# Half of the branch product moved between the steps of the sparse attention, with its gated chunks kept in DRAM, and a new order of some MLP work

## The chip, the cores and the metric

The kernel runs as one program on one core of a Trainium2 chip. The metric is the device time of one execution in microseconds (us). Before the change three runs gave 1763.05, 1754.05 and 1754.68 us, with a median of 1754.68 us. The profiled execution took 1753.3 us.

## The reference, cut to what matters

The program is one decoder layer on 1040 positions (16 meta tokens and 1024 of the input), with a width of 1024. A normalised input is projected; stick-breaking attention (8 heads, "SB") and indexer-selected sparse attention (8 heads, "DS") run on it; their outputs go through one branch matrix each, are gated per channel, summed and projected; then comes a squared-ReLU MLP.

```python
    o_sb = jnp.transpose(o_sb, (1, 0, 2, 3, 4)).reshape(b, tp, SB_W).astype(h.dtype)
    o_ds = jnp.transpose(o_ds, (1, 0, 2, 3, 4)).reshape(b, tp, DSA_W).astype(h.dtype)
    gates = jax.nn.sigmoid(jnp.concatenate([g_sb, g_ds], axis=-1) + b_gate)
    gate_sb, gate_ds = gates[..., :D_MODEL], gates[..., D_MODEL:]
    merged = gate_sb * (o_sb @ w_branch_sb) + gate_ds * (o_ds @ w_branch_dsa)
    return merged @ w_out
...
        h = h + rms_norm(mix, g_mix_post[l])
        ff = sq_relu_mlp(rms_norm(h, g_mlp_pre[l]), w_mlp_in[l], w_mlp_out[l])   # u = relu(h @ w1); (u * u) @ w2
        h = h + rms_norm(ff, g_mlp_post[l])
```

Only `gate_sb * (o_sb @ w_branch_sb)` is moved in time by the change. It needs the SB heads alone, and these are finished before the DS heads start.

## The kernel before, in words

Every matrix product is made to near fp32 accuracy by three passes: each operand is split into a rounded part (`_hi`) and the rest (`_lo`), and TensorE adds hi·hi, hi·lo and lo·hi into one PSUM bank. ScalarE writes the `_hi` parts, and GpSimd or VectorE subtracts to get the `_lo` parts. Weights come in units of 128 x 1024 numbers (512 KB): SyncE loads one (`load_unit`), ScalarE rounds it (`round_unit`), GpSimd takes the rest (`rest_unit`). There are two buffers for them.

The second block of the program holds the projections and the attention. Its order is written out by hand as steps j = 0 to 132, and every engine has its own loop over the same steps. A job is one head and one block of 128 queries; the eight blocks of a head come in the order 7, 0, 6, 1, 5, 2, 4, 3, so a head is eight steps. Steps 0 to 63 start the SB jobs, steps 64 to 127 the DS jobs; head g starts in step 8g. In a step TensorE does, in this order: the scores of job j (`scores`, lines 759 and 760, in two PSUM banks that VectorE empties at line 1163), products of weights and values (`product`, line 810), projection work in the first 64 steps (`project`), the transposes of the weights of job j-2 (`turn`, line 775), once per head the transposes of the next head's values (`values`, line 741), more projection work, and more products. The groups of transposes take turns in PSUM banks 4, 5, 6, and from step 66 on bank 0 too (`tp_take`). ScalarE rounds each group out of its bank (line 932), VectorE takes the rest (line 1192), and the bank is free then. From step 64 on TensorE has no projection work between these.

SyncE issues all DMAs of the block in one queue, in order, and its waits hold back all that stand behind them. `load_head` brings queries, keys and values of a head by eight DMAs and stands in the step after the one that starts the head before. The SB outputs lie in DRAM in two halves; at the steps RELOAD[p] (70, 80, 90, 100) SyncE loads two halves for a pair of heads in `o_raw` (line 648), GpSimd adds them in the step after (line 681), ScalarE rounds the sum at the end of the third step after (`reload`, line 967), GpSimd takes the rest (line 684), and only then may the next pair be loaded, since the buffer is the same.

The third block starts with the branch product: for each of eight chunks k of 128 channels TensorE runs 48 matmuls of 512 columns (24 for SB, 24 for DS; line 344). VectorE multiplies both results by their gates (lines 1891 and 1892), GpSimd adds them (line 1529), ScalarE rounds the sum, and VectorE takes the rest (line 1897). Then come the output projection with norms and residual (lines 1578 and 1596), and the MLP. Both MLP products are made with seven smaller products in place of eight (Strassen-Winograd), so sums of weights and of results are made beside them. The first is a loop over k = 0 to 55 (`inner`, line 1651, 12 matmuls each), the second a loop over i = 0 to 27 (`outer`, line 1674, 48 matmuls each, in four tiles). In both each engine works down its own list. `inner_add` (line 2021) adds a result out of PSUM, `f_sums` (lines 2032 to 2035) makes sums for the second product, `fourth_raw` (lines 2005 and 2007) a difference of activations, `diff_rest` (line 1538, GpSimd) its `_lo` part, `outer_add` (line 2121) adds a tile into `acc`, `last_norm` (lines 2132, 2126, 2136) scales a finished row block of the upper half, and `right_gain`, `left_gain` and `final_row` do so for the lower half.

Of the kernel before, what the change touches and what calls it, by code (L numbers as in the profile page):

```python
# [20 lines left out]
P = 128  # L21
# [23 lines left out]
U_BRANCH, U_OUT, U_MLP = 43, 51, 59  # L45
# [82 lines left out]
RELOAD = [NJ // 2 + 6 + 10 * p_ for p_ in range(4)]  # L128
# [11 lines left out]
def tp_take(key, j):  # L140

    ring = (4, 5, 6) if j < NJ // 2 + 2 else (4, 5, 6, 0)
    TPN[key] = len(TP_BANK)
    TP_BANK.append(min(ring, key=lambda b: max([n for n, x in enumerate(TP_BANK) if x == b], default=-1)))
# [107 lines left out]


# [21 lines left out]
def build(nc, x, meta, w_units, b_gate, g_pre, g_post, g_mlp_pre, g_mlp_post, ident, strict, fill,  # L275
          rope_i, rope_d, out):
    with ExitStack() as ctx:
# [21 lines left out]
        h1_d = nc.dram_tensor("h1_d", (SEQ, D), F32, kind="Internal").ap()  # L299
# [18 lines left out]

        raw_landed = [sem("raw_landed0"), sem("raw_landed1")]
# [137 lines left out]
        o_raw = [at(f"o_raw{s}", [P, SEQ], F32, O_STAGE + 4096 * s) for s in range(2)]  # L457
        q_st = [at(f"q_st{s}", [P, SEQ], F32R, O_QK + s * QK_SET) for s in range(2)]
# [32 lines left out]
        with ExitStack() as st:  # L491
# [6 lines left out]
            qi_in = [sem(f"f_qiin{h}") for h in range(HI)]  # L498
# [11 lines left out]
            op_hi, op_lo = sem("f_ophi"), sem("f_oplo")  # L510
            def pt_of(buf, j, tiles):
# [24 lines left out]
            def _(sp):  # L536
# [66 lines left out]
                for u in range(U_STEP):  # L603
# [15 lines left out]
                    if u == 8:  # L619
                        for v in (5, 6, 7):  # L620
                            in_dram(v)
                        load_head(0)
                for j in range(NJ + 5):
                    for u in STARTS[j]:
                        load_unit(sp, u + 2, u % 2)
                    for part in range(2):
                        for n in ENDS[j][part]:
                            store(n)
                    for k in OUT_AT[j]:
# [21 lines left out]
            def _(pool):  # L651
# [25 lines left out]
                for j in range(NJ // 2 + 1, NJ + 6):  # L677
# [7 lines left out]
                    for p in range(3):  # L685
                        if j == PAIR_AT[p]:
                            pool.wait_ge(op_hi, p + 1)
                            pool.tensor_tensor(o_lo[:, 4 + p, :], o_pair[p][:], o_hi[:, 4 + p, :].bitcast(F32), ALU.subtract).then_inc(op_lo, 1)

            @block.tensor  # L690
            def _(pe):
# [9 lines left out]
                def project(n, kt):  # L701
# [10 lines left out]
                    if kt == KT - 1:  # L712
                        mm.then_inc(pj_done, 1)

# [116 lines left out]
                for j in range(NJ + 5):  # L831
# [4 lines left out]
                    for n, kt in FILL[j][0]:  # L836
                        project(n, kt)
                    if 2 <= j < NJ + 2:
# [5 lines left out]
                    for n, kt in FILL[j][1]:  # L844
                        project(n, kt)
                    for k, slots in PRODUCTS[j][1]:
# [8 lines left out]
            def _(act):  # L855
# [108 lines left out]

                def reload(p):
# [9 lines left out]
                for j in range(NJ + 5):  # L975
# [4 lines left out]
                    for n in ENDS[j][0]:  # L980
                        evacuate(n)
                    if 2 <= j < NJ + 2:
# [5 lines left out]
                    for n in ENDS[j][1]:  # L988
                        evacuate(n)
                    for p in range(4):  # L990
# [11 lines left out]
            def _(dve):  # L1002
# [168 lines left out]
                def scale_pair(p):  # L1171
# [4 lines left out]
                    for half in range(2):  # L1176
# [5 lines left out]
                        else:  # L1182
                            dve.tensor_copy(r_last[:, cols], src).then_inc(tp_free, 1)
# [11 lines left out]
                def rest_values(g):  # L1195
                    for half in range(2):
# [3 lines left out]
                        dve.tensor_tensor(v_hl[dst], src, v_hl[value_parts(g, half, n, 0)[0]].bitcast(F32), ALU.subtract).then_inc(tp_free, 1)  # L1200

# [23 lines left out]
                for j in range(NJ + 6):  # L1225
# [6 lines left out]
                    if j < NJ + 5:  # L1232
                        for n in ENDS[j][0]:
                            rest(n)
                    due += SEARCH[j][0]
# [11 lines left out]
                    if j < NJ + 5:  # L1247
                        for n in ENDS[j][1]:
                            rest(n)
                    due += SEARCH[j][1]  # L1250
# [68 lines left out]
        with ExitStack() as st:  # L1319
# [13 lines left out]
            u_in = [sem(f"m_u{r}") for r in range(RING)]  # L1333
# [40 lines left out]
            def _(sp):  # L1374
                for k in range(KT):
                    if k >= 2:
                        sp.wait_ge(br_free, k - 1)
                    for t in range(2):
                        sp.dma_start(gate[:, k % 2, t], g_d[t * D + k * P:t * D + (k + 1) * P, :]).then_inc(g_in5[k % 2], 16)
                    load_unit(sp, U_BRANCH + k + 2, (U_BRANCH + k) % 2)  # L1380
                for v in range(V0, V0 + 6):
                    load_ring(sp, v)
                sp.wait_ge(br_free, KT)
# [141 lines left out]
            def _(pool):  # L1525
                for k in range(KT):
                    if k < KT - 1:
                        pool.wait_ge(br_free, k + 1)
# [726 lines left out]
```

## Time and profile before

| | |
|---|---|
| median of three runs | 1754.68 us |
| profiled execution | 1753.3 us, of which span 1751.5 us |
| TensorE busy | 1636.0 us (93%), 8360 matmuls |
| VectorE, ScalarE, GpSimd busy | 1235.8, 851.4 and 539.7 us (71%, 49%, 31%) |
| granted TensorE clock, mean | 0.974 |
| DS steps | from 722.5 to about 912.9 us of the span |
| branch product | from 912.9 to 1002.3 us |
| second MLP product | from 1425.3 us, last matmul at 1741.9 us |

Times in the trace are counted from the start of the span. The busy time of TensorE holds the modelled tail of each matmul, so short waits hide in it; the distance between the starts of two matmuls shows more. Where a row has square brackets at its end, they give how long the engine was idle before it, and what it waited for.

### The profile page before, as it was taken

The numbers are of one execution on the slowest core, as the hardware profiler recorded it, in microseconds if no ns is written. First come the engines' busy times: TensorE is split into PE (matmuls) and PEld (weight loads), VectorE is DVE, ScalarE is ACT, GpSimd is POOL, SyncE is SP. The second block draws the span as 40 slices with busy tenths as digits, with TensorE's granted clock in tenths as the row PEclk, the third lists the DMA queues.
The fourth block names the chain that finished last, engine by engine and source line by source line (L and its number), as shares of the span: only waits on it lengthen the run. The fifth ranks groups of instructions, "written<-read, shape, count | busy, mean of one in ns | idle before, by whom it ended". The sixth has DMA issues, their size and how long they took to land. (4 is left out here: it accounts for less than half of the span.)

```text
span 1751.5 us, 23454 instructions
## 1 busy us (share of the span) xinstructions
PE 1636.0 (93%) x8360; PEld 1380.7 (79%) x8360; DVE 1235.8 (71%) x1966; ACT 851.4 (49%) x1650; POOL 539.7 (31%) x332
## 2 busy tenths in 40 slices
PE   4989899999999999888889999899999989999996
PEld 4889888799877777777778878678888868888884
DVE  5287798898888999688863445854544458777876
ACT  5366555555445455577751243645555543333333
POOL 1111254555434435321103440765555500000000
PEclk6999999999999999999989999999999999999998
DMA  4564434344334333355313352234444365453443
GB/s 174 156 190 129 126 117 134 114 130 113 97 96 113 95 94 111 103 118 134 86 50 139 126 201 98 73 138 147 165 170 144 115 242 190 156 169 121 168 143 96
DMA packets 101372, 231.23 MB, mean 132 GB/s; under 512 B 11192, under 2 KB 25848, under 8 KB 101256
## 3 DMA queue, kind: packets, MB, share of 16 engines
q1 hardware_dynamic: 100680, 227.64, 40.8%
q0 software_dynamic: 576, 2.10, 0.7%
q8 instruction: 67, 1.10, 0.3%
q14 instruction: 49, 0.40, 0.1%
HBM read 155.83 MB, written 73.86 MB: 131 GB/s over the span
## 5 line engine op out<-in xcount | busy, mean ns | idle before, releaser
L710 PE MATMUL bk<-x_hi,w_hi 128*128 128x512 f32 (+2 forms) x832 | 308.7, 371 | 1.2 <-PEq L353 1.2
L710 PE MATMUL bk<-x_lo,w_hi 128*128 128x512 f32 (+2 forms) x832 | 299.2, 360 | 0.0
L710 PE MATMUL bk<-x_hi,w_lo 128*128 128x512 f32 (+2 forms) x832 | 298.5, 359 | 0.0
L666 POOL TENSOR_TENSOR pt_lo<-a_buf,pt_hi 128x512 fp32r<-128x512 f32 (+3 forms) x104 | 138.4, 1347 | 193.0 <-ACT pt_hi L930 192.8
L334 POOL TENSOR_TENSOR w_lo<-w_raw,w_hi 128x1024 fp32r<-128x1024 f32 x53 | 130.3, 2459 | 190.9 <-ACT w_hi L330 190.7
L1674 PE MATMUL bank<-v_hi,f_hi 128*128 128x512 f32 x448 | 175.4, 391 | 9.8 <-DVE acc L2121 7.9
L1087 DVE TENSOR_SCALAR_CACHE_REDUCE counted<-sc,small 128x272 uint8<-128x272 f32 (+6 forms) x217 | 182.5, 891 | 0.9
L1674 PE MATMUL bank<-v_hi,f_lo 128*128 128x512 f32 x448 | 174.9, 390 | 0.0
L1674 PE MATMUL bank<-v_lo,f_hi 128*128 128x512 f32 x448 | 174.8, 390 | 0.0
L710 PEld LDWEIGHTS bk<-x_hi,w_lo 128*128 128x128 f32 x832 | 158.5, 191 | 17.6
L710 PEld LDWEIGHTS bk<-x_hi,w_hi 128*128 128x128 f32 x832 | 159.1, 191 | 16.1 <-issue 1.3
L710 PEld LDWEIGHTS bk<-x_lo,w_hi 128*128 128x128 f32 x832 | 158.8, 191 | 13.3
L810 PE MATMUL bk<-pt_hi,v_hl 128*128 128x256 f32 (+2 forms) x384 | 111.5, 315 | 10.1 <-ACT o_st L949 5.7
L1542 POOL TENSOR_TENSOR s_lo<-s,s_hi 128x512 fp32r<-128x512 f32 x64 | 93.8, 1468 | 80.4 <-ACT s_hi L1718 80.4
L1192 DVE TENSOR_TENSOR pt_lo<-bk,pt_hi 128x512 fp32r<-128x512 f32 (+2 forms) x120 | 62.4, 553 | 72.1 <-ACT pt_hi L932 70.9
L1674 PEld LDWEIGHTS bank<-v_hi,f_hi 128*128 128x128 f32 x448 | 84.5, 189 | 28.6 <-DVE acc L2121 8.3
L929 ACT COPY a_buf<-bk 128x512 f32<-128x512 f32 (+3 forms) x104 | 54.3, 522 | 107.3 <-PE bk L775 107.3
L775 PE MATMUL bk<-idf,a_buf 128*128 128x128 f32 (+1 forms) x704 | 102.4, 281 | 4.1 <-DVE pt_lo L1192 2.5
L1542 POOL TENSOR_TENSOR s_lo<-u_raw,s_hi 128x512 fp32r<-128x512 f32 x48 | 67.4, 1409 | 123.5 <-ACT s_hi L1718 123.3
L1143 DVE TENSOR_TENSOR_SCAN n_buf<-n_buf 128x1040 f32<-128x1040 f32 (+3 forms) x64 | 101.8, 1591 | 2.3 <-ACT n_buf L906 2.3
L1651 PE MATMUL bank<-m_hi,s_hi 128*128 128x512 f32 x256 | 99.9, 390 | 1.1 <-DVE m_lo L1938 1.1
L1559 POOL DMA_DIRECT2D out<-scaled x4 | 3.6, 896 | 315.8 <-DVE scaled L2136 315.8
(228 smaller groups left out, 3911.3 us busy)
## 6 DMA issues: line engine op xcount, KB each, us to landing
w_raw<-w_units SPq DMA_DIRECT2D x57, 512.0 KB, 3.8
f_raw<-f_d SPq DMA_DIRECT2D x28, 1024.0 KB, 5.0
u_raw<-w_units SPq DMA_DIRECT2D x32, 512.0 KB, 4.6
f_d<-f_s SPq DMA_DIRECT2D x64, 256.0 KB, 2.3
b<-w_units SPq DMA_DIRECT2D x16, 1024.0 KB, 7.5
f_d<-c SPq DMA_DIRECT2D x48, 256.0 KB, 2.1
k_hi<-k_d SPq DMA_DIRECT2D x32, 260.0 KB, 5.7
k_lo<-k_d SPq DMA_DIRECT2D x32, 260.0 KB, 6.3
```

Of the source, the lines that this page charges most:

```text
L334: pool.tensor_tensor(w_lo[:, s], w_raw[:, s], w_hi[:, s].bitcast(F32), ALU.subtract).then_inc(lo_done, 1)
L666: pool.tensor_tensor(pt_of(pt_lo, j, tiles), raw, pt_of(pt_hi, j, tiles).bitcast(F32), ALU.subtract).then_inc(sb_lo, 1)
L710: mm = pe.matmul(pj[b][:, 0:c1 - c0], w[:, s, kt, :], a[:, kt, c0:c1], start=kt == 0 and k == 0, stop=kt == KT - 1 and k == 2)
L775: mm = pe.transpose(bk[TP_BANK[n]][0:r, m * P:(m + 1) * P], a_buf[:, j % 3, col:col + r], idf[:])
L810: mm = pe.matmul(dst, v_hl[0:r, g % 2, slot, :], w[0:r, cols], start=slot == 0 and w is hi, stop=slot == o + 1 and w is lo)
L929: act.copy(a_buf[:, j % 3, 512 * k:512 * k + m * P].rearrange("p (c k) -> p c k", c=m), src)
L1087: op(dve.tensor_scalar(counted[:, blk(b)], sc[:, blk(b)], cand[:, j:j + 1], None, ALU.is_ge, ALU.add, accum_out=cnt[:, j:j + 1]))
L1143: dve.tensor_tensor_scan(n[:, ::-1], n[:, ::-1], n[:, ::-1], 1.0, ALU.mult, ALU.bypass).then_inc(scan_done, 1)
L1192: dve.tensor_tensor(pt_of(pt_lo, j, tiles), bk[TP_BANK[n]][:, 0:m * P].rearrange("p (c k) -> p c k", c=m), pt_of(pt_hi, j, tiles).bitcast( ...
L1542: pool.tensor_tensor(s_lo[k % RING][:], first_raw(*FIRST[k]), s_hi[k % RING][:].bitcast(F32), ALU.subtract).then_inc(s_lo_done, 1)
L1651: mm = pe.matmul(dst, w[r][:, n, :], b, start=p in (1, 2, 5) and n == 0 and i == 0, stop=n == HT - 1 and i == 2, skip_group_check=True)
L1674: mm = pe.matmul(dst, a[r][:, q, t * P:(t + 1) * P], w[r][:, q, :], start=p in (1, 5, 2) and q == 0 and n == 0, stop=q == QP - 1 and n == ...
```

## The change: what it does

The weight units of the branch product are cut in another way: units 43 to 46 hold the SB matrix and 47 to 50 the DS matrix, each unit two chunks of 128 channels. The SB half becomes 16 parts m (a chunk k = m // 2 and a half c = m % 2 of the positions) of 12 matmuls each, cut in four pieces h of three. The 64 pieces are dealt evenly over the 76 half steps of steps 88 to 125, one in a half step at most, between scores, transposes and products. All parts use PSUM bank 0, so the transposes of the whole second half turn in banks 4, 5 and 6 only. VectorE multiplies a finished part by its gate (`gate_part`, 512 columns) into a buffer, and SyncE stores it in DRAM (`m1_d`) and loads the gate of the part after the next. TensorE starts part m only when part m-1 is gated. RELOAD becomes 70, 74, 78, 82, since all SB outputs are needed at step 88. Four roundings and rests of units move there too. The third block runs 24 matmuls per chunk. It loads `m1_d` in place of the SB gate, and the sum moves from GpSimd to VectorE.

In the MLP `diff_round(2, ...)` goes from k = 4, 5 to k = 6, 7, `fourth_raw` waits until GpSimd has made the rest of the second difference, `inner_add` goes ahead of `f_sums`, `t_sums(1)` goes from k = 52 to 54, and at the end `last_norm` goes from behind the tiles of product 25 to behind those of product 26, and the four `right_gain` behind them.

```diff
-RELOAD = [NJ // 2 + 6 + 10 * p_ for p_ in range(4)]
+RELOAD = [NJ // 2 + 6 + 4 * p_ for p_ in range(4)]
...
-    ring = (4, 5, 6) if j < NJ // 2 + 2 else (4, 5, 6, 0)
-    TP_BANK.append(min(ring, key=lambda b: ...))
+    TP_BANK.append(min((4, 5, 6), key=lambda b: ...))
...
+PARTS = 2 * KT
+B_STEPS = [(j_, part_) for j_ in range(RELOAD[3] + 6, NJ - 2) for part_ in range(2)]
...
+                def store_part(m):
+                    u, k, c = part_at(m)
+                    sp.wait_ge(part_gated, m + 1)
+                    sp.dma_start(m1_d[k * P:(k + 1) * P, c * HALF:(c + 1) * HALF], m1_st[:, m % 2]).then_inc(m1_out[m % 2], 16)
+                    if m + 2 < PARTS:
+                        load_gate(m + 2)
...
+                def branch_part(m, h):
+                    u, k, c = part_at(m)
+                    if h == 0:
+                        if m == 0:
+                            pe.wait_ge(or_lo, 4)
+                            bank_read(NC_ALL - 2 + NC_ALL % 2)
+                        else:
+                            pe.wait_ge(part_gated, m)
+                        pe.wait_ge(lo_done, u + 1)
+                    for n, (w, a) in enumerate(((w_hi, o_hi), (w_hi, o_lo), (w_lo, o_hi))):
+                        mm = pe.matmul(bk[0][:], w[:, u % 2, 4 * (k % 2) + h, :], a[:, h, c * HALF:(c + 1) * HALF], start=h == 0 and n == 0,
+                                       stop=h == 3 and n == 2)
...
+                def next_unit(m):
+                    u = part_at(m)[0]
+                    if m % 4 == 3:
+                        act.wait_ge(part_mm, m + 1)
+                        round_unit(act, u + 2, u % 2, (u + 2) // 2)
...
+                def gate_part(m):
+                    dve.wait_ge(gate_sb_in[m % 2], 16 * (m // 2 + 1))
+                    if m >= 2:
+                        dve.wait_ge(m1_out[m % 2], 16 * (m // 2))
+                    dve.wait_ge(part_mm, m + 1)
+                    dve.tensor_tensor(m1_st[:, m % 2], bk[0][:], gate_sb[:, m % 2], ALU.mult).then_inc(part_gated, 1)
...
-                    dve.tensor_tensor(gated[:, k % 2, 0], bank[2 * (k % 2)][:], gate[:, k % 2, 0], ALU.mult)
-                    dve.tensor_tensor(gated[:, k % 2, 1], bank[2 * (k % 2) + 1][:], gate[:, k % 2, 1], ALU.mult).then_inc(br_free, 1)
+                        dve.tensor_tensor(gated[:, k % 2, 0], bank[2 + k % 2][:], gate[:, k % 2, 1], ALU.mult).then_inc(br_free, 1)
+                        dve.wait_ge(br_free, k + 1)
+                        dve.tensor_tensor(gated[:, k % 2, 0], gated[:, k % 2, 0], gate[:, k % 2, 0], ALU.add).then_inc(add_done, 1)
...
-                    dve.wait_ge(t_rest, REST_NO[0, h])
+                    dve.wait_ge(t_rest, REST_NO[1, 1])
...
                     for t in range(QP):
                         outer_add(i - 1, t)
-                        if i - 1 == N2 - 3 and t:
-                            last_norm(t - 1)
-                        if i - 1 == N2 - 2 and t:
-                            dve.wait_ge(acc_done, 4 * (N2 - 2) + t)
-                            right_gain(t + 3)
+                        if i - 1 == N2 - 2:
+                            last_norm(t)
```

The order of the instructions shows three places. TensorE, steps 88 and 89 (the first two of head 11), before: scores against 344 and 144 keys, and the transposes of `a_buf`.

```order
L759 MATMUL bk<-k_hi_352,q_st_350 128x344
L760 MATMUL bk<-k_lo_354,q_st_350 128x344
L775 MATMUL bk<-idf,a_buf 16x128
L775 MATMUL bk<-idf,a_buf 128x128 x5
L759 MATMUL bk<-k_hi_352,q_st_350 128x144
L760 MATMUL bk<-k_lo_354,q_st_350 128x144
```

The same place now, with pieces of part 0 (`o_hi`, `o_lo` against `w_hi`, `w_lo`):

```order
L817 MATMUL bk<-k_hi_354,q_st_352 128x344
L818 MATMUL bk<-k_lo_356,q_st_352 128x344
L768 MATMUL bk<-o_hi,w_hi 128x512
L768 MATMUL bk<-o_lo,w_hi 128x512
L768 MATMUL bk<-o_hi,w_lo 128x512
L833 MATMUL bk<-idf,a_buf 16x128
L833 MATMUL bk<-idf,a_buf 128x128 x5
L768 MATMUL bk<-o_hi,w_hi 128x512
L768 MATMUL bk<-o_lo,w_hi 128x512
L768 MATMUL bk<-o_hi,w_lo 128x512
L817 MATMUL bk<-k_hi_354,q_st_352 128x144
L818 MATMUL bk<-k_lo_356,q_st_352 128x144
```

Three matmuls stand ahead of the transposes and three behind them. SyncE's queue, before, from the last loads of head 11 (`v_raw`) to the first of head 12:

```order
L594 DMA v_raw<-v_d 64x528
L595 DMA v_raw<-v_d 64x512
L591 DMA q_st_349<-q_d 64x1024
L592 DMA k_hi_351<-k_d 64x1040
L593 DMA k_lo_353<-k_d 64x1040
```

The same place now:

```order
L612 DMA v_raw<-v_d 64x528
L613 DMA v_raw<-v_d 64x512
L687 DMA o_raw_347<-o_d 64x1024 x2
L687 DMA o_raw_348<-o_d 64x1024 x2
L643 DMA gate_sb<-g_d 128x512 x2
L334 DMA w_raw<-w_units 128x1024
L648 DMA m_d<-m_st 128x512
L643 DMA gate_sb<-g_d 128x512
L609 DMA q_st_351<-q_d 64x1024
L610 DMA k_hi_353<-k_d 64x1040
```

The fourth reload, two gates, a weight unit and the store of part 0 now stand ahead of head 12. VectorE behind product 25 of the second MLP product, before (`acc` is `outer_add`, `scaled` is `last_norm`, `v_lo` and `f_lo` are operands of product 27):

```order
L2121 TENSOR_TENSOR acc<-acc,bank 128x512 x2
L2132 TENSOR_SCALAR small<-small 128x1
L2126 RECIPROCAL small<-small 128x1
L2136 SCALAR_TENSOR_TENSOR scaled_12242<-acc,small,g_fin 128x1024
L2121 TENSOR_TENSOR acc<-acc,bank 128x512
...
L2136 SCALAR_TENSOR_TENSOR scaled_12245<-acc,small,g_fin 128x1024
L2052 TENSOR_TENSOR v_lo_12228<-t_12234,v_hi_12226 128x1024
L2055 TENSOR_TENSOR f_lo_12224<-f_raw_12220,f_hi_12222 128x1024
```

The same place now:

```order
L2208 TENSOR_TENSOR acc<-acc,bank 128x512 x4
L2139 TENSOR_TENSOR v_lo_12596<-t_12602,v_hi_12594 128x1024
L2142 TENSOR_TENSOR f_lo_12592<-f_raw_12588,f_hi_12590 128x1024
...
L2208 TENSOR_TENSOR acc<-acc,bank 128x512
L2219 TENSOR_SCALAR small<-small 128x1
L2213 RECIPROCAL small<-small 128x1
L2223 SCALAR_TENSOR_TENSOR scaled_12610<-acc,small,g_fin 128x1024
```

The operands of product 27 now come ahead of the four `last_norm`.

## Rows read from the trace of the kernel before

**Rows 1.** The page: GB/s in 40 slices; the chain that ended last, by line
```profile
GB/s 174 156 190 129 126 117 134 114 130 113 97 96 113 95 94 111 103 118 134 86 50 139 126 201 98 73 138 147 165 170 144 115 242 190 156 169 121 168 143 96
...
PE bank L1674 16%; PE bank L1651 15%; PE bank L344 5%; PE bank L1578 3%; POOL s_lo L1542 1%; POOL row_lo L1533 1%; POOL t_lo L1538 1%; DMA b<-w_units 1%; DMA f_raw<-f_d 0%; PE bank L1596 0%; DMA u_raw<-w_units 0%; DVE f_lo L2055 0%; DVE s L1964 0%; DVE acc L2121 0%; DMA w_raw<-w_units 0%
```

**Rows 2.** Windows: busy time (count) of each engine, granted clock, DMA share, GB/s
```profile
791.30:897.10 105.80, 91.53 (x623) 76.62 (x622) 84.40 (x234) 73.81 (x177) 14.22 (x6) 0.95 0.41 91
912.90:1002.30 89.40, 89.40 (x386) 73.82 (x387) 35.18 (x23) 15.86 (x16) 33.17 (x14) 0.98 0.43 153
1098.50:1153.20 54.70, 44.45 (x179) 35.10 (x178) 45.69 (x48) 31.43 (x54) 43.15 (x22) 0.91 0.22 79
```

**Rows 3.** Timeline of TensorE in the branch product: start, duration, engine, line
```profile
950.83 0.62 PE L344 MATMUL bank<-o_lo,w_hi 128*128 128x512 f32 x2
951.28 0.61 PE L344 MATMUL bank<-o_hi,w_lo 128*128 128x512 f32 x2
```

**Rows 4.** Timeline of VectorE and GpSimd in the branch product
```profile
915.21 1.23 DVE L1887 TENSOR_TENSOR o_lo<-o_pair,o_hi 128x1024 fp32r<-128x1024 f32 x1 [1.11 <-ACT o_hi L1735]
937.04 1.23 DVE L1891 TENSOR_TENSOR gated<-bank,gate 128x1024 f32<-128x1024 f32 x1 [2.62 <-PE bank L344]
941.82 2.40 POOL L334 TENSOR_TENSOR w_lo<-w_raw,w_hi 128x1024 fp32r<-128x1024 f32 x1
942.98 2.32 DVE L1897 TENSOR_TENSOR m_lo<-gated,m_hi 128x1024 fp32r<-128x1024 f32 x1 [3.58 <-ACT m_hi L1744]
```

**Rows 5.** Waits of TensorE, steps 88 to 125: us in total, times, longest
```profile
PE bk L759 <- DVE small L1163: 8.2, 6, 1.6
PE bk L785 <- DVE pt_lo L1192: 2.7, 2, 1.3
PE bk L775 <- DVE pt_lo L1192: 1.7, 2, 0.8
```

**Rows 6.** Timeline of TensorE, projection matmuls right behind transposes
```profile
712.13 0.48 PE L710 MATMUL bk<-x_hi,w_hi 128*128 128x512 f32 x1
712.45 0.40 PE L710 MATMUL bk<-x_lo,w_hi 128*128 128x512 f32 x1
```

**Rows 7.** Timeline: last load of head 12's values, and their transposes
```profile
794.57 0.60 SPq L595 DMA_DIRECT2D v_raw<-v_d  x1
...
804.82 0.53 PE L741 MATMUL bk<-idf,v_raw 64*16 64x64 f32 x9
```

**Rows 8.** Timeline of SyncE, GpSimd and ScalarE around the second reload
```profile
757.86 2.36 SPq L648 DMA_DIRECT2D o_raw<-o_d  x4
764.85 2.39 POOL L681 TENSOR_TENSOR o_raw<-o_raw,o_raw 128x1024 f32<-128x1024 f32 x1 [7.09 <-DMA o_raw<-o_d]
755.38 2.38 POOL L684 TENSOR_TENSOR o_lo<-o_raw,o_hi 128x1024 fp32r<-128x1024 f32 x1 [5.55 <-ACT o_hi L967]
764.30 0.63 ACT L916 ACTIVATE a_buf<-n_buf,small 128x400 f32<-128x400 f32 x1 [1.28 <-DVE small L1163]
```

**Rows 9.** Timeline at the start of the MLP
```profile
1125.77 6.66 POOL L1538 TENSOR_TENSOR t_lo<-t_raw,t_hi 128x1024 fp32r<-128x1024 f32 x2
1133.72 0.80 PE L1651 MATMUL bank<-t_hi,s_hi 128*128 128x512 f32 x1 [4.13 <-POOL s_lo L1542]
1148.79 0.47 PE L1651 MATMUL bank<-t_hi,s_hi 128*128 128x512 f32 x1 [4.10 <-issue]
```

**Rows 10.** Timeline between the two MLP products
```profile
1421.61 0.68 DVE L2021 TENSOR_TENSOR c<-bank,c 128x512 f32<-128x512 f32 x1
1435.20 1.05 ACT L1732 CAST f_hi<-f_raw 128x1024 fp32r<-128x1024 f32 x1 [7.52 <-DMA f_raw<-f_d]
1437.77 0.47 PE L1674 MATMUL bank<-v_hi,f_hi 128*128 128x512 f32 x1 [1.45 <-DVE f_lo L2055]
```

**Rows 11.** Timeline of the end
```profile
1724.26 1.22 DVE L2052 TENSOR_TENSOR v_lo<-t,v_hi 128x1024 fp32r<-128x1024 f32 x1
1729.54 0.79 PE L1674 MATMUL bank<-v_hi,f_hi 128*128 128x512 f32 x1 [7.89 <-DVE acc L2121]
1734.20 0.69 DVE L2121 TENSOR_TENSOR acc<-acc,bank 128x512 f32<-128x512 f32 x1 [0.27 <-PE bank L1674]
```

More of the change, by code:

```diff
@@ L497, in build @@
             ki_in, wt_t, wt_done = sem("f_kiin"), sem("f_wtt"), sem("f_wtok")
-            qi_in = [sem(f"f_qiin{h}") for h in range(HI)]
+            landed = [sem(f"landed{h}") for h in range(HI)]
+            qi_in = landed
             s_ready, s_relu, s_acc, search_op = (sem("f_" + n) for n in ("sready", "srelu", "sacc", "search"))
@@ L628, in _ @@
                             store(n)
+                        for m in B_ENDS[j][part]:
+                            store_part(m)
                     for k in OUT_AT[j]:
@@ L1332, in build @@
             t_rounded, t_rest, t4_raw = (sem("t_" + n) for n in ("trnd", "trest", "t4raw"))
-            u_in = [sem(f"m_u{r}") for r in range(RING)]
+            u_in, QI_LANDED = landed[:RING], 64
             w_sum, s_hi_done, s_lo_done, product, copied, added = (sem("m_" + n) for n in ("wsum", "shi", "slo", "prod", "copy", "add"))
@@ L1525, in _ @@
             def _(pool):
-                for k in range(KT):
-                    if k < KT - 1:
-                        pool.wait_ge(br_free, k + 1)
-                        pool.tensor_tensor(gated[:, k % 2, 0], gated[:, k % 2, 0], gated[:, k % 2, 1], ALU.add).then_inc(add_done, 1)
-                    rest_unit(pool, U_BRANCH + k + 2, (U_BRANCH + k) % 2)
+                for u in range(U_BRANCH_DS, U_OUT):
+                    rest_unit(pool, u + 2, u % 2)
                 for v in range(V0, U_MLP):
@@ L2177, in _ @@
                                 final_row(t + 3)
-                    if i - 1 == N2 - 3:
-                        last_norm(3)
                     if i - 1 == N2 - 2:
-                        dve.wait_ge(acc_done, 4 * (N2 - 1))
-                        right_gain(NB - 1)
+                        for t in range(4, NB):
+                            dve.wait_ge(acc_done, 4 * (N2 - 2) + t - 3)
+                            right_gain(t)
                 final_row(NB - 1)
@@ L2220 @@
     units += [unit(w_in, 3368 + P * j) for j in range(2 * KT)]
-    branches = np.concatenate([f(w_branch_sb)[0], f(w_branch_dsa)[0]], axis=0)
-    units += [unit(branches, P * j) for j in range(KT)]
+    for branch in (f(w_branch_sb)[0], f(w_branch_dsa)[0]):
+        units += [unit(np.concatenate([branch[:, 2 * P * j:2 * P * j + P], branch[:, 2 * P * j + P:2 * P * j + 2 * P]], axis=0), 0) for j in range(4)]
     units += [f(w_out)[0][P * j:P * j + P] for j in range(KT)]
```

110 lines of the change are left out of this document (79 added, 31 removed).

## The prediction

> **What bounds the kernel now.** First the page. In its chain by line, TensorE's product lines carry nearly all of what lies behind the attention; the branch product alone (L344) is 5% of the span, some 88 us [rows 1]. Then the windows, one row per stage [rows 2]. Through the branch product TensorE is busy for all of 89.4 us while VectorE has 35.2 us of work: TensorE is the bound, and a matmul removed there is time saved. In steps 88 to 125 (791.3 to 897.1 us) TensorE is busy for 91.5 of 105.8 us at a granted clock of 0.95, VectorE for 84.4: nobody is the bound alone, a chain goes round the engines. The waits of TensorE there are for the scores' statistics on VectorE (8.2 us), the rests of `r_wide` (2.7) and of the weights (1.7) [rows 5]. They sum to 12.6 us, but the modelled tail of a matmul hides short waits. Walking the starts of one head's eight steps I find some 4.4 us by which they come later than the work before them needs; the stretch holds 38 steps, some 4.8 heads and their edges, about 22.5 us in all (an estimate; its floor is the 14.3 us that the window shows idle). So TensorE's own work there is about 83 us.
>
> **The branch block.** 192 of its 384 matmuls of 512 columns go. In the steady part six take three pairs' time, and pairs start 0.45 us apart (950.83, 951.28) [rows 3]: 0.227 us each. 192 × 0.227 = 43.5 us. Does TensorE still pace it? Two chunks (48 matmuls) will take 10.9 us. VectorE then has, per two chunks, two each of: a product out of PSUM (1.23), the sum that GpSimd did, and a rest (1.23 as `o_lo` took) [rows 4]; with 1.23 for the sum, of the same shape, 7.4 us. GpSimd has one `w_lo` of 2.40 us, and `m_lo`, starting beside one, took 2.32 in place of 1.23 [rows 4]. Should VectorE be held for a whole one every two chunks it needs 9.8 us, still under 10.9. DMA: before, a chunk took 1.5 MB in 11 us; now it takes two half-MB gates and half a unit, 1.3 MB in 5.5 us, about 230 GB/s; the page has slices of 242 and 201 [rows 1], so it holds, without much room. Term −43.5 (end on the bad side −39, if one load in four is late by a microsecond).
>
> The Trainium skill ("SBUF — State Buffer", section "Who interferes with whom") says that a VectorE instruction with two SBUF inputs contends with a GpSimd instruction that reads SBUF, and that whoever issues first blocks the other for its whole length. The row with 2.32 agrees. It speaks against moving the sum, which has two SBUF inputs, to VectorE; by it the 7.4 us become up to 12.2 if every second two-input instruction met a `w_lo`, but there is only one `w_lo` for two chunks, which the 9.8 already pays.
>
> **The fill, steps 88 to 125.** 64 pieces of three such matmuls. Behind transposes a first one of 512 columns took 0.32 us to the next start (712.13 to 712.45) and not 0.23 [rows 6], so a piece costs 3 × 0.227 + 0.07 to 0.09 = 0.75 us, 48 us for all. Own work plus pieces: 83.3 + 48 = 131. If every wait of today is covered the stretch goes from 105.8 to 131 us. What is late next:
> - One bank holds all parts, so TensorE waits at piece 0 of part m for VectorE's gate of part m-1. The deal leaves a free half step at 12 of 76 places only; at about 11 of the 15 changes the next part follows in the next half step, with a score pair or a step's transposes between. VectorE needs 0.69 us for the gate, behind evictions and rests. I take 0.5 us for each: 5 us (ends 0 and 24). Behind the waiting piece stand the transposes, and for those ScalarE's roundings and the products.
> - Head 12's values. Their last load was issued at 794.57 and they were transposed without a wait at 804.82 [rows 7]. Now `load_head(12)` stands behind the store of part 0, whose last piece is in step 89, gated near 798 us; eight issues of some 0.6 us follow [rows 7] and then about 6 us to land, so near 809, where TensorE, slowed by the pieces, wants them at about 808. Head 15 likewise stands behind the store of part 10. With the queries and keys that come a step later I take 6 us for all (ends 0 and 12).
> - Cover gives the clock back: 0.95 in this stretch [rows 2]; with shorter idle times, 1.0 of 131 us would be −6; I take −3 (ends 0 and −6).
>
> VectorE gets 16 gates of 0.69, 11 us, to 95 of 139; ScalarE four roundings of 1.06: neither becomes the bound. Sum: 131 + 5 + 6 − 3 = 139, a term of +33 us. Ends: +22 (no new wait) and +67 (half of today's waits stay, 11 us, and each change of part costs 1.6 us: 48 + 24 + 6 − 11). I take a value near the low one, because the waits of today are at fixed places (the third score chunk, `r_wide`) and the pieces stand right ahead of those places.
>
> The Trainium skill ("TensorE: Matmul & The Clock Gate", section "HAM oscillation — how this bites in real kernels") holds that idle times between bursts of matmuls bring the clock down and that work kept dense keeps it up. By it the fill would bring the full 6 us. The trace shows 0.95 here against 0.98 in the dense branch product, whose start is slow. That points the same way by half as much.
>
> **Reloads four steps apart, ring of three.** One reload is a closed chain, since `o_raw` is shared: issues from 757.86, landed 764.85 (7.0 us), sum 2.39, rounding 1.04, rest 2.38 (as at 755.38) [rows 8]: 12.8 us. Four steps of this part take about 11 us. So each of the three later ones is late: for the second, ScalarE ends `exponent(77)` near 765.0 (its last statistic starts at 764.30) and finds the sum about 2.3 us later, at 767.24, and the later ones lose 0.7 and 1. While ScalarE waits, transposes stay unrounded and TensorE runs into its ring, which has three banks now. Term +5 with the ring (ends +1 and +9).
>
> **MLP.** At its start GpSimd's two `diff_rest` take 6.66 us beside `fourth_raw` on VectorE, and TensorE waits 4.13 us before product 10 and 4.10 before 13 [rows 9]; the stretch is 54.7 us long at a clock of 0.91 for 179 matmuls [rows 2], 40 us of work. Afterwards the two no longer meet: product 10 comes about 3 us sooner, 12 waits for the later second difference, and 14 follows `inner_add` that no longer stands behind 5 us of `f_sums`. −4.5 (ends 0 and −7). Between the products, `inner_add` at 1421.61 moves ahead of three `f_s` and can go at once; the first product of `outer` follows 4 us sooner, but `f_raw` at 1435.20 came by DMA [rows 10] and sets a floor: −3.5 (ends −0.5 and −4.5). At the end `v_lo` for product 27 ran at 1724.26, behind four `last_norm`, and TensorE waited 7.89 us until 1729.54 [rows 11]. Without them it follows at once. VectorE is then the later one: adds and `last_norm` of about 2.6 us four times and `right_gain` of 3 us put the first add of product 27 at about 1730, where it was at 1734.20, and a wait of 1.3 behind it goes. −5 (ends −3 and −7).
>
> **Sum.** −43.5 + 33 + 5 − 4.5 − 3.5 − 5 = −18.5 us, from the profiled 1753.3 (span 1751.5 and 1.8 around it), which lies 1.4 us under the median of the runs. I round the gain down by two, because a chain that I walked leaves out small waits: 1737 us against the median. Called faster is what is over 0.5%, 8.8 us, under 1754.68, which is about what a measurement can tell: under 1746.
>
> **Rivals.**
> - *Fill well hidden* (chance 0.15): no gate wait and no late values. For it: VectorE is only 80% busy. Against: its order is fixed. The fill costs 22: −43.5 + 22 + 5 − 13 = −29.5, 1724 us.
> - *Given back, no change* (0.23): half of today's waits stay beside the pieces, as they come from a chain that the pieces also delay (scores, statistics, exponent, transposes). For it: pieces stand ahead of `turn`. Fill 48 − 11 + 11 = 48: −43.5 + 48 + 5 − 13 = −3.5, 1750 us.
> - *Slower* (0.12): the single bank. A gate stands behind a whole half step's work of VectorE, and TensorE stops at each of 15 changes for 1.6 us: fill +67, in all +15.5, 1769 us. It decides from about 1.1 us a change on, if half of the waits of today stay. For it: VectorE already keeps TensorE waiting at scores [rows 5]. Against: most changes have transposes or scores between.
> - That the SB half doesn't leave the branch block can't be: its matmuls are gone there.
>
> Forecast 0.50, with its own range 1730 to 1746. Range of 8 in 10: 1722 to 1757, reaching over most of the first two rivals; unknown ends (fill −11 to +34, reload ±4, MLP ±4) fill it. Faster takes the forecast's case and the first rival, 0.65; same 0.23; slower 0.12.
>
> **What would show it.** In windows of the new trace: the branch block near 46 us with TensorE busy throughout; steps 88 to 125 near 139 us with a clock of 0.97 or more; steps 64 to 87 longer by 5. In the waits of TensorE there: those for `m1_st` (the gate) near 5 us, for `v_raw` near 6, and those for the scores' statistics under 4. On ScalarE, waits for `o_raw` of 2.3, 0.7 and 1. No wait before product 27. I am wrong if the score waits stay at 8 us or more, if gate waits pass 12 us, or if the branch block is above 52 us.

## The result and the profile after

| | before | after |
|---|---|---|
| median of the runs | 1754.37 us | 1765.95 us |
| profiled span | 1751.5 us | 1766.0 us |

The change makes the kernel slower: the ratio of the times is 1.0063, with a 95% interval of 1.0035 to 1.0092. The forecast was 1737 us.

The spans differ by 14.5 us. Cut at the starts of steps and of blocks, the difference is made up as follows:

| stretch | before | after | measured | forecast |
|---|---|---|---|---|
| up to step 64 | 722.53 | 723.72 | +1.2 | 0 |
| steps 64 to 87 | 68.8 | 75.4 | +6.6 | +5 |
| steps 88 to 123 | 100.7 | 158.7 | +58.0 | +33, with the next row |
| step 124 to the branch block | 20.9 | 23.6 | +2.7 | |
| branch block | 89.2 | 46.0 | −43.1 | −43.5 |
| output projection, norms | 96.5 | 97.5 | +1.0 | 0 |
| first MLP product | 326.8 | 322.2 | −4.6 | −4.5 |
| second, to the end | 326.2 | 318.9 | −7.3 | −8.5 |

All terms are near but one, the dealt pieces: +60.7 where +33 was forecast. (The two MLP rows split the forecast of the middle part at another place than its terms do; see below.) The windows of the changed kernel (columns as in [rows 2]); the second row answers to the first row of [rows 2], the third to its second:

```profile
723.72:799.12 75.40, 62.00 (x397) 52.46 (x395) 48.30 (x137) 52.09 (x119) 25.90 (x14) 0.91 0.61 139
...
799.12:957.81 158.69, 134.64 (x775) 109.17 (x776) 91.91 (x241) 72.69 (x173) 13.33 (x6) 0.92 0.40 111
981.36:1027.40 46.04, 46.04 (x192) 37.89 (x193) 32.52 (x22) 11.60 (x11) 7.17 (x3) 0.94 0.66 246
```

In the last row TensorE is busy for all of the 46.04 us: it paces the branch block, and the 246 GB/s were to be had. In the row above, the same 36 steps of before took this:

```profile
791.31:891.98 100.67, 87.26 (x595) 73.11 (x594) 80.02 (x223) 69.92 (x168) 14.22 (x6) 0.95 0.43 96
```

TensorE is busy 47.4 us longer for 180 more matmuls, and its idle time (the length of the stretch less its busy time) grew from 13.4 to 24.1 us. The waits of TensorE in steps 88 to 123 after the change (compare [rows 5]):

```profile
PE bk L799 <- DMA v_raw<-v_d: 11.8, 3, 5.5
PE bk L817 <- DVE small L1235: 7.6, 6, 1.8
PE bk L768 <- DVE m_st L1280: 5.0, 7, 1.2
PE bk L799 <- DVE pt_lo L1265: 0.6, 1, 0.6
```

The gate waits (L768) are the 5 us of the forecast. The values come late by 11.8 us, not 6, and the score waits (L817) are what they were, 7.6 us against 7.8 in the same steps of before: no piece covered them. The waits for the rests of `r_wide` and of the weights (4.4 us in [rows 5]) are down to the 0.6 of the last row. SyncE's timeline shows how the first late head comes about:

```profile
807.45 0.32 SPq L648 DMA_DIRECT2D m_d<-m_st  x1
...
808.90 0.45 SPq L609 DMA_DIRECT2D q_st<-q_d  x1
...
814.08 0.60 SPq L613 DMA_DIRECT2D v_raw<-v_d  x1
```

SyncE waited until VectorE had gated part 0 (from 806.74 to 807.4), and only then issued the eight loads of head 12. TensorE's timeline at the same place:

```profile
814.53 0.39 PE L768 MATMUL bk<-o_hi,w_hi 128*128 128x512 f32 x1
814.75 0.39 PE L768 MATMUL bk<-o_lo,w_hi 128*128 128x512 f32 x1
...
819.85 0.76 PE L799 MATMUL bk<-idf,v_raw 64*16 64x64 f32 x9 [3.60 <-DMA v_raw<-v_d]
...
823.08 0.63 PE L768 MATMUL bk<-o_lo,w_hi 128*128 128x512 f32 x1
823.51 0.63 PE L768 MATMUL bk<-o_hi,w_lo 128*128 128x512 f32 x1
```

Ahead of the wait two matmuls of a piece start 0.22 us apart, behind it 0.43: the idle 3.6 us brought TensorE down from 2.4 to 1.2 GHz. The windows of four steps each show this level in the granted clock, here of steps 88 to 91 and 92 to 95, and of steps 112 to 115 and 116 to 119:

```profile
799.12:813.82 14.70, 13.67 (x81) 11.13 (x82) 9.75 (x28) 7.53 (x20) 1.42 (x1) 1.00 0.55 163
813.82:834.00 20.18, 16.58 (x92) 13.50 (x91) 9.83 (x26) 7.11 (x19) 0.00 (x0) 0.83 0.37 95
...
903.07:917.18 14.11, 13.46 (x82) 11.08 (x81) 8.90 (x27) 7.60 (x20) 0.00 (x0) 1.00 0.42 119
917.18:938.81 21.63, 16.05 (x96) 13.08 (x95) 11.30 (x28) 8.60 (x19) 4.74 (x2) 0.84 0.47 131
```

The rows with clock 1.00 take 14.7 and 14.1 us (11.8 and 10.7 before), the two with a late head 20.2 and 21.6 (10.2 and 11.8 before). Not all of the low clock stands behind a late head. Here the last waits had been 0.56 and 0.79 us, and the matmuls of a piece start 0.42 us apart:

```profile
891.10 0.80 PE L768 MATMUL bk<-o_hi,w_hi 128*128 128x512 f32 x1 [0.79 <-DVE m_st L1280]
891.70 0.63 PE L768 MATMUL bk<-o_lo,w_hi 128*128 128x512 f32 x1
892.12 0.63 PE L768 MATMUL bk<-o_hi,w_lo 128*128 128x512 f32 x1
```

On ScalarE the waits for `o_raw` are there, 3.6 us in all over three reloads. Before product 27 TensorE waits no more, where it waited 7.89 us [rows 11].

### The profile page after: what moved, and what is told of

Read it like the earlier page. It is cut to its first block and busy times, and to the rows that moved or that the text cites. A ratio compares the mean times of both kernels' runs of the same rounds, so it can differ in the third digit from the quotient of the medians.

```text
span 1766.0 us, 23532 instructions
## 1 busy us (share of the span) xinstructions
PE 1645.1 (93%) x8360; PEld 1385.7 (78%) x8360; DVE 1260.7 (71%) x1981; ACT 852.1 (48%) x1650; POOL 523.0 (30%) x325
## 5 line engine op out<-in xcount | busy, mean ns | idle before, releaser
L753 PEld LDWEIGHTS bk<-x_hi,w_lo 128*128 128x128 f32 x832 | 158.7, 191 | 17.6
L753 PEld LDWEIGHTS bk<-x_lo,w_hi 128*128 128x128 f32 x832 | 159.0, 191 | 13.4
L1265 DVE TENSOR_TENSOR pt_lo<-bk,pt_hi 128x512 fp32r<-128x512 f32 (+2 forms) x120 | 62.4, 553 | 96.5 <-ACT pt_hi L994 95.8
L868 PEld LDWEIGHTS bk<-pt_hi,v_hl 128*128 128x128 f32 (+1 forms) x384 | 75.4, 196 | 30.8 <-issue 11.8
```

The costliest lines, as they stand in the source:

```text
L753: mm = pe.matmul(pj[b][:, 0:c1 - c0], w[:, s, kt, :], a[:, kt, c0:c1], start=kt == 0 and k == 0, stop=kt == KT - 1 and k == 2)
L868: mm = pe.matmul(dst, v_hl[0:r, g % 2, slot, :], w[0:r, cols], start=slot == 0 and w is hi, stop=slot == o + 1 and w is lo)
L1265: dve.tensor_tensor(pt_of(pt_lo, j, tiles), bk[TP_BANK[n]][:, 0:m * P].rearrange("p (c k) -> p c k", c=m), pt_of(pt_hi, j, tiles).bitcast( ...
```

## The experiments

Twelve kernels ran. "Stretch" is the length of steps 88 to 123 in the one profiled execution of each. The kernels of e8 to e11 leave out part of the SB half and don't compute the layer.

| kernel | us | stretch | clock in it |
|---|---|---|---|
| before | 1754 | 100.7 | 0.95 |
| after | 1766.0 | 158.7 | 0.92 |
| MLP edits alone (e1) | 1742.0 | 100.8 | 0.95 |
| loads first (e2) | 1754.1 | 146.2 | 0.96 |
| late loads in before (e3) | 1773.2 | 121.1 | 0.84 |
| reloads 4 apart in before (e4) | 1761.3 | 102.7 | 0.92 |
| e2, piece inside the scores (e5) | 1751.2 | 141.9 | 0.99 |
| e5, free half steps behind parts (e6) | 1749.6 | 141.4 | 0.96 |
| e6, reloads 5 apart (e7) | 1754.6 | 139.5 | 1.00 |
| e2 without the pieces' work (e8) | 1729.9 | 126.4 | 0.85 |
| e6, small gates (e9) | 1743.1 | 133.9 | 1.00 |
| e8, small gates (e10) | 1722.0 | 116.0 | 0.90 |
| e6, ScalarE copies parts (e11) | 1744.6 | 136.4 | 0.99 |
| e7, head 11 first (e12) | 1752.6 | 141.2 | 0.99 |

**e1, the MLP edits alone.** In the kernel before:

```diff
+                    if k in (6, 7):
+                        diff_round(2, k - 6)
...
+                    if p in (2, 7, 3):
+                        inner_add(k)
...
+                        if i - 1 == N2 - 2:
+                            last_norm(t)
```

> The kernel before with the MLP part of the change alone (diff_round, fourth_raw, inner_add, t_sums, last_norm and right_gain). Theory: these edits are worth what the two traces show behind the attention, -4.6 us in the first MLP product and -7.3 us from there to the end, so about 1742.5 us, and they owe nothing to the rest. Rival: part of that came from the other timing of the weight loads ahead of them, and alone they give half, about 1748 us.

1741.98 us, ratio 0.9934 (0.9913 to 0.9955): the theory. The MLP part is worth 12 us alone, and all the rest of the change costs 24 us on top of it (1766 − 1742). Of all kernels here that compute the layer this is the fastest, ahead of both before and after.

**e2, loads ahead of the parts' stores.**

```diff
                 for j in range(NJ + 5):
+                    if j >= NJ // 2 + 24 and j % NB == 0 and j // NB + 1 < 2 * H:
+                        load_head(j // NB + 1)
...
-                    if j % NB == 1 and j // NB + 1 < 2 * H:
+                    if j < NJ // 2 + 24 and j % NB == 1 and j // NB + 1 < 2 * H:
```

> The changed kernel with load_head of heads 11 to 15 as the first thing of the step that starts the head before (step 80, 88, ...), ahead of gates, units and the stores of parts. Theory: TensorE's 11.8 us of waits for v_raw in steps 88 to 125 go, and with them most of the low clock behind them (0.83, 0.91, 0.84 in their stretches; some 7 us), so 1766 goes to about 1748 us (-15 to -20). Rival: the time of the dealt pieces is lost in the single bank and in the score waits; something else is late right behind v_raw, and no more than 5 us come back.

The edit took in heads 12 to 15 (steps 88 to 112); head 11 stayed where it was. 1754.13 us, 12 us under the changed kernel and level with before (ratio 1.0, 0.9988 to 1.0011). The stretch and its waits:

```profile
799.52:945.72 146.20, 130.93 (x776) 106.88 (x776) 91.92 (x241) 72.87 (x173) 11.93 (x5) 0.96 0.44 120
```

```profile
PE bk L819 <- DVE small L1237: 6.8, 5, 1.8
PE bk L770 <- DVE m_st L1282: 4.6, 6, 1.2
PE bk L801 <- DVE pt_lo L1267: 3.0, 4, 1.3
```

The waits for values are gone, and TensorE's busy time fell from 134.6 to 130.9 us for the same matmuls, as the clock rose from 0.92 to 0.96. But waits for `pt_lo` at the transposes of values rose from 0.6 to 3.0 in their place, and low clock showed with no late head: 0.72 from 865.5 to 871.5 and 0.74 from 913.5 to 919.5. So late loads explain 12 us of the loss, less than the 15 to 20 of the theory, and far more than the rival's 5.

**e3, late loads with no piece in sight.**

```diff
+                        if g in (12, 13, 15):
+                            sp.wait_ge(z_ready, Z_END[8 * (g - 1) + 2])
                         load_head(g)
```

> The kernel before, with SyncE holding the loads of heads 12, 13 and 15 until the scores two steps later are done. No piece of the branch product is dealt here. Theory: three waits for v_raw of some 4 us each, and a granted clock near 0.85 in the four steps that follow each one where it was 1.00, some 2 us more for each: +17 us, 1771. Rival: idle time of such a length costs itself only, no clock: +11 us or less.

1773.24 us, 19 us over before (ratio 1.011, 1.0088 to 1.0132): the theory, if with longer waits than it said.

```profile
PE bk L743 <- DMA v_raw<-v_d: 17.9, 3, 7.0
PE bk L761 <- DVE small L1165: 7.2, 5, 1.6
```

```profile
791.07:912.17 121.10, 93.55 (x595) 79.91 (x594) 80.94 (x223) 70.29 (x168) 14.23 (x6) 0.84 0.35 80
```

Beside 17.9 us of waits TensorE is busy 93.6 us for the matmuls that took 87.3 before, as the clock fell from 0.95 to 0.84; the waits for `r_wide` and weights (4.4 us) went into the new ones, but for 0.8. The Trainium skill ("TensorE: Matmul & The Clock Gate", section "HAM oscillation — how this bites in real kernels") says that waits for data between bursts of matmuls bring the clock down, and that the bursts behind them start slow; these rows agree. What I made of it in the prediction, a clock given back by the pieces, left out that the change brings such waits itself. (e8 below shows the other side: with the pieces' work in them the same steps have a clock of 0.96, without it 0.85.)

**e4, reloads four steps apart, ring of four kept.**

```diff
-RELOAD = [NJ // 2 + 6 + 10 * p_ for p_ in range(4)]
+RELOAD = [NJ // 2 + 6 + 4 * p_ for p_ in range(4)]
```

> The kernel before with the reloads at steps 70, 74, 78, 82 in place of 70, 80, 90, 100, and the ring of four banks kept. Theory: a reload is a chain of about 13 us in a place for 11, ScalarE waits for o_raw, and steps 64 to 87 become 5 to 6 us longer, 1760 us, with the granted clock of steps 76 to 79 down from 1.00. Rival: the ring of three banks made the +6.6 us, and this gives +1 or nothing.

1761.27 us (ratio 1.0032, 1.0018 to 1.0047). Steps 64 to 87, and ScalarE's waits for the sum there:

```profile
722.32:796.84 74.52, 60.24 (x396) 50.63 (x395) 47.87 (x136) 52.03 (x119) 25.87 (x14) 0.91 0.63 146
```

```profile
ACT o_hi L967 <- POOL o_raw L681: 5.1, 3, 2.3
```

74.5 us against 68.8 before and 75.4 in the changed kernel: the crowded reloads make 5.7 of the 6.6 us, the ring of three at most the other 0.9. In the stretch e4 takes 102.7 us, 2.0 more than before. The low clock came in steps 80 to 83 (0.74), hardly in 76 to 79 (0.97).

**e5, a piece inside the wait.** To e2, in TensorE's `scores`:

```diff
                     for m, (c0, c1) in enumerate(ZCH[i]):
+                        if m == 2:
+                            for m_, h_ in B_FILL[j][0]:
+                                branch_part(m_, h_)
```

> The kernel of e2_loads_first, and in the first step of a head the piece that stood behind the scores now stands between the second and the third score chunk, where TensorE waits for VectorE. Theory: a piece covers a wait of today only if it stands between the two instructions that the wait divides; then the 6.8 us of score waits in steps 88 to 123 fall to under 2 us, and 1754 becomes about 1748 us. Rival: the waits belong to a chain that goes round the engines, and come back at the next rest or gate: 1753 us or more.

1751.16 us (0.9973 to 1.0005 of before): between the two, and 3 us under e2 (0.9988 to 1.0011), which the intervals don't part for certain. The score waits fell from 6.8 to 3.7 us, and the gate waits rose from 4.6 to 6.4:

```profile
PE bk L770 <- DVE m_st L1285: 6.4, 7, 1.8
PE bk L822 <- DVE small L1240: 3.7, 4, 1.1
PE bk L801 <- DVE pt_lo L1270: 3.0, 4, 1.3
```

**e6, free half steps behind the parts.** To e5:

```diff
-    j_, part_ = B_STEPS[n_ * len(B_STEPS) // (4 * PARTS)]
+    j_, part_ = B_STEPS[n_ + n_ // 4 * (len(B_STEPS) - 4 * PARTS) // (PARTS - 1)]
```

> The kernel of e5_score_fill, with the free half steps of the deal put behind the last pieces of 12 parts, where they were spread evenly over pieces. Theory: the gate waits, 4.6 us over six changes of part in e2_loads_first, fall to under 1.5 us, 3 us off the time of e5. Rival: with no free half steps elsewhere the other engines get their transposes later, and nothing is won.

1749.64 us, half of the 3 us of the theory under e5, which their intervals don't part (0.9956 to 0.9989 here); the runs of e6 (1747.4 to 1751.4) and of e2 (1751.3 to 1757.2) hardly overlap. Gate waits fell to 2.8 us, score waits rose to 4.9:

```profile
PE bk L822 <- DVE small L1240: 4.9, 5, 1.7
PE bk L801 <- DVE pt_lo L1270: 3.7, 4, 1.3
PE bk L770 <- DVE m_st L1285: 2.8, 3, 1.2
```

Both times about half of what was covered came back as another wait on VectorE. That points to a chain that goes round through it; e9 puts it to the test.

**e7, reloads five apart.** To e6, `4 * p_` in `RELOAD` becomes `5 * p_`.

> The kernel of e6_gaps_at_parts with the reloads five steps apart (70, 75, 80, 85), and the deal from step 91 on. Theory: five steps give a reload's chain of 13 us its room, ScalarE no longer waits for o_raw, and the 5 to 6 us of steps 64 to 87 come back: e6 less 4, near 1741 us, level with the MLP edits alone. Rival: the shorter stretch for the 64 pieces has only 6 free half steps, gate waits come back, and the time stays that of e6.

1754.61 us, 5 us worse than e6, not 8 better. ScalarE's waits for `o_raw` (4.5 us in e6) are gone, as the theory had it, and yet steps 64 to 87 took 81.4 us, against 74.9 in e6; the stretch behind them is 1.9 us shorter. SyncE issued the third reload at 777.71 us, as soon as the second was through, and the loads of head 11 behind it, the last at 785.07; TensorE then waited 3.9 us for the values:

```profile
PE bk L801 <- DMA v_raw<-v_d: 3.9, 1, 3.9
```

**e12, head 11 first too.** To e7, `NJ // 2 + 24` of e2's edit becomes `NJ // 2 + 16`.

> The kernel of e7_reload5 with head 11's loads, too, at the start of their step 80, ahead of the third reload's wait. Theory: e7 lost its gain to a wait of 3.9 us for v_raw in step 84, as SyncE stood at the reload, and to the low clock behind it; that goes, 1755 becomes 1747 us, a little under e6. Rival: the later and denser deal itself cost e7 its gain: 1752 us or more.

1752.57 us, by its number the rival (1752 or more), but not for its reason. Now the eight loads of head 11 stand ahead of the reload, its sum is late, and ScalarE waits for it in the same steps, with the rounding of the transposes behind it:

```profile
PE bk L801 <- DVE pt_lo L1270: 4.1, 1, 4.1
```

```profile
ACT o_hi L1040 <- POOL o_raw L722: 2.2, 1, 2.2
```

Whichever of the two goes first, the other is late, and TensorE waits as long (3.9 and 4.1 us). The steps there still take 18.05 us at a clock of 0.72, as in e7 (18.07).

**e8, the pieces without their work.** To e2; eleven of the twelve matmuls of a part are left out, so the SB half is not computed:

```diff
+                    if h < 3:
+                        return
-                    for n, (w, a) in enumerate(((w_hi, o_hi), (w_hi, o_lo), (w_lo, o_hi))):
+                    for n, (w, a) in enumerate(((w_hi, o_hi),)):
```

> The kernel of e2_loads_first with 11 of the 12 matmuls of each part left out (one, of the last piece, is kept, so every gate, store, unit and semaphore stays); it does not compute the SB half rightly. Theory: what the fill costs is the pieces' own time on TensorE with the clock, so steps 88 to 123 fall from 146 us to about 103, against 100.7 before: some 42 us for 176 matmuls (0.24 each), hardly covered by anything, 1712 us. Rival: gates, units and the one bank lengthen the steps by themselves, and the stretch stays above 110 us.

1729.88 us: the rival. The stretch takes 126.4 us with 12 matmuls more than before in it, 25.7 us over before:

```profile
799.15:925.52 126.37, 104.41 (x607) 87.39 (x608) 89.90 (x240) 72.17 (x171) 13.34 (x6) 0.85 0.50 139
```

The clock is 0.85, and TensorE busy 104.4 us where 87.3 did before. So what comes along with the pieces (gates, units, stores, the order) lengthens the steps by itself. Against e2, 169 matmuls are missing in the stretch, 38.4 us by 0.227 each, and they add only 19.8. Where the other 18.6 go, the two windows tell: with the work in, TensorE's idle time falls from 22.0 to 15.3 us, and its busy time rises by 26.5 only, as the clock goes from 0.85 to 0.96. So the pieces do cover waits and do give the clock back, but mostly those that their own company brings.

**e9 and e10, small gates.** To e6 and to e8; the gate product takes 16 of 512 columns (the rest of the SB half is not gated, and the store reads the same buffer, `o_raw[1]`):

```diff
-                    dve.tensor_tensor(m1_st[:, m % 2], bk[0][:], gate_sb[:, m % 2], ALU.mult).then_inc(part_gated, 1)
+                    dve.tensor_tensor(o_raw[1][:, (m % 2) * HALF:(m % 2) * HALF + 16], bk[0][:, 0:16], gate_sb[:, m % 2, 0:16], ALU.mult).then_inc(part_gated, 1)
```

> The kernel of e6_gaps_at_parts with each gate product on VectorE over 16 columns in place of 512 (the other columns of the SB half are not gated), all waits, stores and loads kept. Theory: in the sparse steps VectorE's work stands in the chain that goes round the engines, so the 10 us that it got are paid in full or nearly: 1750 becomes about 1742 us, and the gate waits nearly go. Rival: VectorE has slack beside the pieces, and only the 2.8 us of gate waits shrink: 1748 us.

> The kernel of e8_pieces_out (11 of 12 matmuls of each part left out) with each gate product over 16 columns in place of 512. Theory: the 126 us that steps 88 to 123 still took there, against 100.7 before, come from VectorE's 10 us in the chain and from the low clock that the longer waits bring; both go for the most part, 108 us, and 1730 becomes about 1713. Rival: the one bank's order and SyncE's queue hold the steps whatever a gate costs: the stretch stays above 120 us.

e9: 1743.14 us, 6.5 under e6: the theory. e10: 1721.99 us, 7.9 under e8, half of what the theory said. The stretches:

```profile
801.19:935.08 133.89, 124.51 (x772) 102.12 (x773) 83.14 (x238) 71.83 (x169) 11.93 (x5) 1.00 0.47 131
```

```profile
798.10:914.09 115.99, 98.23 (x608) 82.13 (x608) 82.85 (x239) 71.19 (x170) 13.35 (x6) 0.90 0.55 151
```

7.0 us less of VectorE's work in each shortened them by 7.5 and 10.4 us. VectorE was busy for only 64% of e6's stretch, and still the gates were paid in full. Not all of it is waiting: in e9 TensorE's idle time is 2.5 us shorter than in e6, and 5.0 us are its busy time for the same 772 matmuls, with the clock at 1.00 where it was 0.96. So a part of the price came by way of the clock; e7, with all gates and a clock of 1.00, takes 5.6 us more than e9, if with another deal.

e10 stays 15.3 us over before: 4.4 us of idle time and 11.0 of busy time, of which its 13 more matmuls explain some 3 us (an estimate, at 0.227 each); the clock is 0.90 against 0.95. No run tells what brings this about: the waits at one place or another, the order through the single bank, or ScalarE's four roundings.

**e11, ScalarE empties the bank** in place of VectorE (to e6; the SB gate is left out):

```diff
+                    act.wait_ge(part_mm, m + 1)
+                    act.copy(m1_st[:, m % 2], bk[0][:]).then_inc(part_gated, 1)
```

> The kernel of e6_gaps_at_parts with ScalarE copying each finished part out of the bank, VectorE doing nothing for it, and the SB gate left out. Theory: VectorE is in the chain and ScalarE less so, 4 to 6 us fewer, 1745 us. Rival: the chain runs through both alike (the scores' exponents and the roundings), and 16 copies of some 0.55 us cost what the gates did: 1749 us or more.

1744.61 us (0.9913 to 0.9959 of before), 5.0 under e6: the theory. VectorE loses 14 gates, 9.6 us, in the stretch, and ScalarE gets 14 copies, 8.2 us; the time falls all the same, so ScalarE's work is worth less here than VectorE's. The gate itself would still have to be paid elsewhere.

## Why the prediction was wrong, step by step

- **The branch block** (−43.5): right, −43.1, with TensorE busy throughout.
- **The MLP** (−13): the sum is right, −11.9 in the trace and −12 alone (e1), its terms less so. The start was forecast at −4.5: product 10 does come 3.8 us sooner (1156.33 less 1124.9, against 1133.72 less 1098.5), but a wait of 5.2 us for `s_lo` follows behind it, and up to the last wait for `c` only 2.5 us are left. Between the products it is −2.3 (forecast −3.5), and from there to the end −7.2 (forecast −5), where the wait of 7.89 us is gone. Two terms too large and one too small cancel, which is luck.
- **Reloads** (+5): right, +6.6, of which e4 gives 5.7 to the spacing. ScalarE's waits were there, 3.6 us.
- **Gate waits** (5): 5.0. The single bank, my rival for "slower", was to cost 24 us in such waits; that was not the cause. That the time it gave (1769) is near is chance. What the order through one bank costs besides these waits is part of what e10 leaves open.
- **The pieces' own time** (0.75 us each, 48 in all): about right. 60 pieces stand in the stretch, 45 us by this price. e2, at nearly the clock of before, is busy 43.7 us longer for 181 more matmuls; the changed kernel, at a lower clock, 47.4 us for 180; e9, at a clock of 1.00, 37.2 us for 177.
- **Cover**, the step that failed first. The prediction took the 22.5 us of waits off in full, "because the waits of today are at fixed places" and "the pieces stand right ahead of those places". Idle time grew from 13.4 to 24.1 us instead. Of its two places the one at `r_wide` was covered (2.7 us before; 0.8 in e2), the third score chunk was not: 7.6 us stayed. That wait lies between two instructions of one step; a piece ahead of the first moves both. Even a piece put between them (e5) won half, and new waits at the transposes of values (3.0 us in e2) came in.
- **"Neither becomes the bound"**, the second. The forecast priced what comes with the pieces by the waits for gates and values alone, and VectorE's and ScalarE's new work at nothing. e8 shows that this company costs 25.7 us in the stretch even with the loads ahead of the stores and nearly no piece's work. Taking 7 us of VectorE's gates out gave their full time back (6.5 us in e9, 7.9 in e10), and moving them to ScalarE gave 5 (e11). That VectorE's gates stand in the round of scores, statistics, transposes and rests is my reading of these runs; the rows show the price, not the path.
- **The values** (6): mis-sized, 11.8 us. Part 0 was to be gated near 798; with the 7.8 us by which step 88 starts later, that is near 806. It was 807.4, and the loads landed near 820, when TensorE had wanted them at 816.2. Three heads (12, 13, 15) were late, where two were priced.
- **The clock** (−3): the wrong sign. It was 0.92, not 0.97: behind each late head TensorE ran at half speed for some four to six microseconds, and now and then behind shorter waits. Moving the loads gave 12 us for waits and clock together (e2), and e3 shows both without any piece. That dense pieces lift the clock was not wrong as such: it is 0.96 in e2 against 0.85 in e8, and 1.00 in e7 and e9. The long waits took more than that gave.

In sum, of the 28 us missed (+60.7 against +33), e2 finds 12, e5 3 and e6 1.5 (neither of these two clear of the noise by itself), and e9 6.5, by leaving work out. The stretch of e9 is 133.9 us, still 33 over before. Its pieces cost 45 us by the price above, so some 12 us of them are covered (an estimate), where 22.5 were forecast. That the rest of the miss is this missing cover is argued, not shown.

None of this makes the deal a gain. The best kernel with it that computes the layer is e6, 1749.6 us, against 1742.0 for the MLP edits alone: from step 64 to the branch block e6 takes 240.8 us and e1 191.3, 49.5 more, for 43 us saved behind it.

What stays open: the 15 us of e10 with hardly any gates' or pieces' work, and how much of e8's low clock comes from which wait. A second bank for the parts was not tried, as all eight are in use.

## What to carry to other kernels

In this kernel filler matmuls ahead of a waiting pair covered nothing of its wait, and between the two instructions that the wait divides about half. Price what comes with them too (an element-wise step, a store in the shared queue): here that cost more than the matmuls' own work added, and 7 us of work on an engine that was 64% busy cost 7. Where a new store goes into a hand-ordered DMA queue, look at what is queued behind it and price its lateness with the clock that the wait costs. Parts of a change that touch different stages should be timed alone: here 12 us of gain hid in a change that lost 12.

## What the runs showed of the hardware

In the changed kernel an idle time of 3.6 us in an otherwise dense TensorE stream was followed by some six microseconds at 1.2 GHz, matmuls of 512 columns starting 0.43 us apart and not 0.22 to 0.23; behind the other two late heads (2.7 and 5.5 us of waiting) it was some four. In e3, behind 7.0 us of waiting, products of 256 columns started 0.21 us apart where 0.12 is usual, until 6.6 us after the wait. Waits of 0.56 and 0.79 us close together (changed kernel, 888 to 891) and one of 1.78 us (e2, at 864.47) were followed by about three microseconds at that level as well, while in the kernel before waits of 1.52 us (at 815.94) and 1.54 us (at 860.40) stand in stretches with a clock of 1.00. What decides between these cases no run shows. The cost shows in TensorE's busy time, beside the wait itself: in e3 93.6 us for the same matmuls as 87.3.
